# Three-way attention: the scores of the unit two ahead are multiplied between a unit's two turnings, no longer in front of the first

## The chip, the cores and the metric

The kernel runs on one core of a Trainium2 chip. The metric is the device time of one execution in microseconds (us); the median of three executions of the kernel before is 3567.4 us (3563.12 to 3571.15). The core has five engines that run side by side, each strictly in its own program order: TensorE (PE, matmuls), VectorE (DVE), ScalarE (ACT), GpSimd (POOL) and SyncE (SP, which issues the loads). They wait for each other by semaphores.

## The reference, cut to what matters

Two blocks of two layers each run on 512 tokens of width 1024. The change lies in both layers of the second block, in the attention with three branches (compressed keys, selected blocks, window). For each of 8 heads:

```
s_c = q . kc * scale + bias     p_c = masked_softmax(s_c)   o_c = p_c . vc      (31 compressed keys)
s_s = q . ks * scale + bias     p_s = masked_softmax(s_s)   o_s = p_s . vs      (selected blocks)
s_w = q . kw * scale + bias     p_w = masked_softmax(s_w)   o_w = p_w . vw      (window)
o   = g0 * o_c + g1 * o_s + g2 * o_w
```

With 512 tokens there are 8 blocks of 64 and 16 may be selected, so every causal block is selected. All is causal: a block of 128 queries number i reads (i + 1) * 128 keys. The result is multiplied by `w_out`, added to the input and normalised.

## The kernel before, in words

**Units.** The attention stage (`pe_nsa`, `dve_nsa`, `act_nsa`) goes over 16 units u = 4 * hp + i: hp is one of 4 pairs of heads (one head of each of two key groups g), i one of 4 blocks of 128 queries. The number of keys, and with it nearly every duration, grows with i.

**What one unit costs each engine, and the names used below.**

- Scores (PE, `scores(u)`, L1970): six products, in the order compressed 0, selected 1, compressed 1, selected 0, window 1, window 0. They fill banks 0 to 4 of PSUM. Each waits until the same bank's scores of the unit before have been read.
- Reads (DVE, L2176): six passes that add the bias, keep the least value and bring the scores to SBUF. The first one needs the first two products.
- Exponentials (ACT, L2218): six, each after its read.
- Norms (DVE, `post(u)`, L2130 to L2143): a reciprocal, two small products, and four scalings, selected first, window after. They need all six exponentials. In the DVE's program the norms of unit u stand behind the reads of unit u + 1.
- First turning (PE, `turn(u, SLC)`, L1980): 2 * (i + 1) transposes of the selected probabilities into banks 5 and 6. The one of group 0 needs the norm of group 0.
- Second turning (PE, `turn(u, WIN)`, L1980): the same for the window, into the same two banks.
- Copy back (ACT, `back(u)`, L2202): each turned group is copied from its bank to SBUF. A turning waits for the copy back of the turning before it in the same bank, so each turning waits for ScalarE unless something stands between. In the ACT's program the copies back of unit u stand behind the exponentials of unit u + 1.

**What else lies in the stage.** Once in four units, in front of the first turning of i = 3, PE turns the compressed probabilities (`turn_cmp`, L1987), and the DVE copies them (`back_cmp`, L2150) ahead of its reads two units later. Behind the first turning of units 4, 8 and 12, and at the end, PE multiplies a head pair's probabilities by the values (`pv`, L1999 and L2008; 64 products and 8 pairs of short ones); ACT and DVE then take the sum (L2208, L2154). Between the two turnings of units 0, 2, 6, 7, 10, 11, 14 and 15 stands an early part of the output projection (`pe_early2`, L281 to L283, twelve products), which the DVE takes from bank 7 (L2064) behind its reads of the unit two later and in front of its norms, with one to three more passes behind the norms. At u = 4, 9 and 13 ACT makes the high part of a weight slot (L319), and POOL then subtracts to get the low part (L329).

**What sets the order.** All queues are written out by hand; no scheduler moves anything. Ahead of the loop of PE stand scores(0), scores(1) and three quarters of the first early part. The products of the output projection (`pe_out2`) follow the last `pv` at once.

Of the kernel before, what the change touches and what calls it, by code (L numbers as in the profile page):

```python
# [73 lines left out]
def build(nc, t):  # L74
    ctx = ExitStack()
    with ctx:
# [1711 lines left out]
        def pe_hgrn_last(eng):  # L1788
            eng.wait_ge(hsq, HG)
            eng.wait_ge(st_ready, 12)  # L1790
            eng.wait_ge(hrs, 2 * HG - 3)
            eng.matmul(bank[7][:, :], onesD, sq[:, (HG - 1) % 2, :], start=True, stop=True).then_inc(hsum, 1)
# [140 lines left out]
        CMP, SLC, WIN = range(3)  # L1933
# [5 lines left out]
        def cw(i):  # L1939
            return 8 * i + 7  # L1940
# [6 lines left out]
        def score_bank(w, g, m):  # L1947
            if w == CMP:
                return bank[4][:, 64 * g:64 * g + m]
            return bank[2 * (w - 1) + g][:, 0:m]  # L1950

        def pe_nsa(eng):
            eng.wait_ge(tp_free, 13)
            eng.wait_ge(dec_exp, 2 * HU)
            eng.wait_ge(a_mask, A_MASKS * HU)
            eng.wait_ge(hout, HG - 1)

            def scores(u):
                hp, i = divmod(u, NT)
                n = (i + 1) * P  # L1960
                if i == 0:
                    eng.wait_ge(tp_free, 13 + hp)
                for o, (w, g) in enumerate(MADE):
                    lo = g * DH
                    keys = (kcmp[lo:lo + DH, 0:cw(i)], projT[lo:lo + DH, KSL, 0:n], projT[lo:lo + DH, KWI, 0:n])[w]
                    if u:
                        eng.wait_ge(p_max, 6 * (u - 1) + FREED[o])
                    if w == CMP and g == 1:
                        eng.wait_ge(s_ready, 6 * u + 1)
                    eng.matmul(score_bank(w, g, cw(i) if w == CMP else n), projT[lo:lo + DH, NQ + hp, i * P:(i + 1) * P],  # L1970
                               keys, start=True, stop=True).then_inc(s_ready, 1)

            def turn(u, w):
                i = u % NT
                for g in range(2):
                    eng.wait_ge(p_norm, 4 * u + 2 * (w - 1) + g + 1)
                    if u or w == WIN:
                        eng.wait_ge(p_back, 4 * u + 2 * (w - 2) + g + 1)
                    for j in range(i + 1):
                        mm = eng.transpose(bank[5 + g][:, j * P:(j + 1) * P], pslot[u % 3][:, w - 1, g, j * P:(j + 1) * P],  # L1980
                                           ident)
                    mm.then_inc(p_turn, 1)

            def turn_cmp(hp):
                eng.wait_ge(c_norm, 4 * hp + 4)
                for m in range(2):
                    mm = eng.transpose(bank[4][:, (2 + m) * P:(3 + m) * P], pslot_c[:, hp % 2, m, :], ident)  # L1987
                mm.then_inc(c_turn, 1)

            def pv(hp):  # L1990
                eng.wait_ge(p_back, 16 * (hp + 1))
                eng.wait_ge(c_back, hp + 1)
                eng.wait_ge(early_out, EARLY_BEFORE[hp])
                o = bank[7]
                for w in range(2):
                    for j in range(NT):
                        for g in range(2):
                            lo = g * DH
                            eng.matmul(o[lo:lo + DH, j * P:S], vg[:, j, w * P + lo:w * P + lo + DH],  # L1999
                                       pT[g][:, w, j, j * P:S], start=(w == 0 and j == 0), stop=False,  # L2000
                                       skip_group_check=True)
                for i in (0, 2, 1, 3):
                    if i == 1:
                        mm.then_inc(c_half, 1)
                        eng.wait_ge(c_half, hp + 1)
                    for g in range(2):
                        lo, row = g * DH, 64 * (i % 2) + 32 * g
                        mm = eng.matmul(o[lo:lo + DH, i * P:(i + 1) * P], vcmp[row:row + cw(i), 0:DH],  # L2008
                                        probC[row:row + cw(i), hp % 2, i // 2 * P:(i // 2 + 1) * P], start=False,
                                        stop=(i == NT - 1), skip_group_check=True)  # L2010
                mm.then_inc(o_ready, 1)

            scores(0)
            pe_hgrn_last(eng)
            scores(1)
            pe_early2(eng, 0, (0, 1, 2))
            eng.wait_ge(hout, HG)
            for u in range(NU):
                if u + 2 < NU:
                    scores(u + 2)  # L2020
                if u % NT == NT - 1:
                    turn_cmp(u // NT)
                turn(u, SLC)
                if u and u % NT == 0:
                    pv(u // NT - 1)
                if u == 0:
                    pe_early2(eng, 0, (3,))
                if u == 1:
                    eng.wait_ge(early_out, 1)
                    eng.matmul(bank[7][:, :], onesD, early2(0), start=True, stop=True).then_inc(mean_out, 1)  # L2030
                if u in EARLY2_AT:
                    pe_early2(eng, EARLY2_AT.index(u) + 1)
                turn(u, WIN)
            pv(NSA // 2 - 1)
# [8 lines left out]
        def early2(m):  # L2043

            return early[:, m, :] if m < 4 else early_more[:, m - 4, :]

        def pe_early2(eng, m, qs=None):

            if m == 1:
                eng.wait_ge(mean_kept, 1)  # L2050
            elif m:
                eng.wait_ge(early_out, m)
            elif qs[0] == 0:
                eng.wait_ge(hrs, 2 * HG - 1)
            for k, hp in enumerate(range(3)):
                if m == 1 + sum(u < 4 * (hp + 1) for u in EARLY2_AT):
                    eng.wait_ge(o_taken, hp + 1)
            pe_tile(eng, bank[7][:, :], n_out2, A2, m, A2_MADE, [guH[:, HQ + h, :] for h in range(HG)],
                    [guH[:, HGT + h, :] for h in range(HG)], qs)
# [334 lines left out]
        for layer in range(DEPTH):  # L2394
            with nc.Block() as block:
# [28 lines left out]
                @block.tensor  # L2424
                def _(pe):
                    pe_turn(pe, 2)
                    pe_proj_N(pe, n_in2 + 3, (1, 3, 4, 5))
                    pe_compress(pe)
                    pe_turn(pe, 3)
                    pe_compress_out(pe)  # L2430
                    for j in range(4, T2_EARLY - 1):
                        pe_turn(pe, j)
                    pe.wait_ge(vp_free, 4)
                    pe_hgrn_turn(pe)
                    pe_turn(pe, T2_EARLY - 1)
                    pe_hgrn_suffix(pe)
                    pe.wait_ge(k_back, HG)
                    pe_proj_N(pe, n_in2 + 12, HV_BANKS)
                    pe.wait_ge(tp_free, T2_EARLY)
                    pe.wait_ge(suf_exp, 3)  # L2440
                    pe_proj_N(pe, n_vg, VG_BANKS, VG, VG_ROWS, taken=(0, 0, 5, 6),
                              between={0: lambda eng: pe_decays(eng, 0), 1: lambda eng: pe_decays(eng, 1)})
                    pe_hgrn(pe)
                    pe_nsa(pe)
                    pe_out2(pe)
                    pe_layer_norm(pe, 0)
                    pe_ffn(pe, 0, n_ffn2, 8, ln_free(1), norm=1)
                    pe_layer_norm(pe, 1)
                    pair_of(pe, n_next2, 16)
# [289 lines left out]
```

## Time and profile before

| | us |
|---|---|
| median of three executions | 3567.4 |
| the profiled execution's own time | 3564.28 |
| its span in the trace | 3562.5 |
| PE busy in the span | 3421.0 (96%) |
| the attention stage in the first layer of the second block | 119.0, from 2290.5 to 2409.5 |
| the same in the second layer | 119.7, from 3018.7 to 3138.4 |
| PE busy in these two | 104.56 and 105.78 |

A row of the timeline gives the start, the duration of the merged instructions, engine, line, operation and how many; in brackets stands how long the engine was idle before it and what it waited for. A row of the stretches gives the length, busy time and count of each engine in the order PE, weight loads, DVE, ACT, POOL, then the granted TensorE clock as a share of full, the DMA share and GB/s. PE is the engine with the most work in the whole kernel and in the stage; the stage is about 3.3% of the span in each of the two layers.

### The profile page before, as it was taken

To read this page: it belongs to the slowest core of one execution; us is meant where nothing else is said; L and a number is where in the kernel's file an instruction comes from. 1 tells how busy PE (TensorE), PEld (TensorE's weight loads), DVE (VectorE), ACT (ScalarE), POOL (GpSimd) and SP (SyncE) were. 2 spreads that over 40 slices of the span, in tenths; PEclk is the share of its full clock that TensorE was granted. 3 is DMA by queue.
4 is the path that set the end of the run, shared out by engine and by line. 5 is a ranking of instruction groups with operands and counts; after the bars stand their busy time and mean duration, and the time that the engine had idled before them with its cause. 6 is when DMAs were issued, how large, how long until landed. Compare 5 with 4: busy or idle time off the path is not lost. (4 is left out here: it accounts for less than half of the span.)

```text
span 3562.5 us, 47692 instructions
## 1 busy us (share of the span) xinstructions
PE 3421.0 (96%) x17380; PEld 2700.5 (76%) x17380; DVE 1617.5 (45%) x2782; ACT 1270.3 (36%) x2154; POOL 1379.8 (39%) x599
## 2 busy tenths in 40 slices
PE   8999999899999999999999999989999999899998
PEld 6888766688878887766788877757888787568886
DVE  4442345644335432363644155774331458743312
ACT  3222345522232222265322244463222344642223
POOL 3444322244434444222344433304444443034444
PEclk9999999999999999999999999999999999999999
DMA  5333321223323233211223332202323322022332
GB/s 176 97 95 97 116 61 41 65 95 94 99 82 96 95 96 122 83 54 40 79 94 99 97 124 73 67 19 74 98 94 98 122 82 75 13 63 97 96 98 96
DMA packets 86341, 308.18 MB, mean 87 GB/s; under 512 B 11157, under 2 KB 11669, under 8 KB 84798
## 3 DMA queue, kind: packets, MB, share of 16 engines
q1 hardware_dynamic: 86206, 306.37, 27.2%
q8 instruction: 87, 1.43, 0.2%
q14 instruction: 48, 0.39, 0.0%
HBM read 301.59 MB, written 4.74 MB: 86 GB/s over the span
## 5 line engine op out<-in xcount | busy, mean ns | idle before, releaser
L329 POOL TENSOR_TENSOR wL<-ring,wH 128x1024 fp32r<-128x1024 f32 (+1 forms) x519 | 1270.1, 2447 | 2120.3 <-ACT wH L319 2023.6
L281 PE MATMUL bank<-hH,wH 128*128 128x512 f32 x2448 | 965.7, 394 | 11.0 <-DVE yT L758 4.8
L283 PE MATMUL bank<-hH,wL 128*128 128x512 f32 x2448 | 954.3, 390 | 0.0
L282 PE MATMUL bank<-hL,wH 128*128 128x512 f32 x2448 | 953.8, 390 | 0.0
L319 ACT ACTIVATE wH<-ring 128x1024 fp32r<-128x1024 f32 (+1 forms) x525 | 551.2, 1050 | 1122.4 <-PE bank L283 939.5
L281 PEld LDWEIGHTS bank<-hH,wH 128*128 128x128 f32 x2448 | 460.3, 188 | 115.6 <-issue 6.3
L283 PEld LDWEIGHTS bank<-hH,wL 128*128 128x128 f32 x2448 | 460.0, 188 | 96.6
L282 PEld LDWEIGHTS bank<-hL,wH 128*128 128x128 f32 x2448 | 460.5, 188 | 94.6 <-issue 1.4
L281 PE MATMUL bank<-guH,wH 128*128 128x512 f32 x1248 | 492.7, 395 | 2.3 <-ACT early L1154 1.4
L283 PE MATMUL bank<-guH,wL 128*128 128x512 f32 x1248 | 487.4, 391 | 0.0
L282 PE MATMUL bank<-guL,wH 128*128 128x512 f32 x1056 | 410.8, 389 | 0.0
L281 PEld LDWEIGHTS bank<-guH,wH 128*128 128x128 f32 x1248 | 235.6, 189 | 56.8 <-issue 3.2
L283 PEld LDWEIGHTS bank<-guH,wL 128*128 128x128 f32 x1248 | 235.2, 188 | 49.5
L647 DVE TENSOR_TENSOR gfull<-bank,work 128x512 f32<-128x512 f32 x88 | 60.8, 691 | 379.9 <-PE bank L283 379.9
L282 PEld LDWEIGHTS bank<-guL,wH 128*128 128x128 f32 x1056 | 198.2, 188 | 41.8 <-issue 1.0
L654 DVE CAST guH<-gfull 128x512 f32 x132 | 213.1, 1614 | 19.6 <-DVE gfull L652 4.1
L358 DVE TENSOR_TENSOR acc<-acc,work 128x512 f32<-128x512 f32 x36 | 74.8, 2079 | 287.9 <-ACT work L541 287.9
L568 ACT ACTIVATE work<-work 128x512 f32<-128x512 f32 x88 | 55.6, 632 | 416.6 <-DVE work L644 416.6
L656 DVE TENSOR_TENSOR guL<-gfull,guH 128x512 f32 x132 | 182.7, 1384 | 16.2
L652 DVE TENSOR_TENSOR gfull<-work,bank 128x512 f32<-128x512 f32 x44 | 30.3, 688 | 301.4 <-PE bank L283 285.0
L744 PE MATMUL bank<-wH,hH 128*128 128x512 f32 (+1 forms) x320 | 119.9, 375 | 2.4 <-DVE yT L758 2.0
L746 PE MATMUL bank<-wH,hL 128*128 128x512 f32 (+1 forms) x320 | 118.3, 370 | 0.0
(290 smaller groups left out, 3879.2 us busy)
## 6 DMA issues: line engine op xcount, KB each, us to landing
ring<-in_w SPq DMA_DIRECT2D x376, 512.0 KB, 3.6
ring<-in_down SPq DMA_DIRECT2D x96, 448.0 KB, 3.3
ring<-in_down SPq DMA_DIRECT2D x48, 512.0 KB, 3.6
ring<-in_next SPq DMA_DIRECT2D x16, 512.0 KB, 3.6
mix<-in_table SPq DMA_DIRECT2D x2, 2560.0 KB
mix<-spread SPq DMA_DIRECT2D x4, 768.0 KB, 6.3
mix<-row SPq DMA_DIRECT2D x1, 2560.0 KB
spread<-mix SPq DMA_DIRECT2D x1, 2560.0 KB, 7.6
```

The source lines that it names most:

```text
L281: eng.matmul(out, a, hi, start=first, stop=False)
L282: eng.matmul(out, a, lo, start=False, stop=False)
L283: return eng.matmul(out, b, hi, start=False, stop=last)
L319: eng.activation(parts_of(n, per)[0][:, 0:width], ring[:, n % NSLOT, 0:width], ACT.Copy).then_inc(w_hi, 1)
L329: eng.tensor_tensor(l[:, 0:width], ring[:, n % NSLOT, 0:width], h[:, 0:width], ALU.subtract).then_inc(w_lo, 1)
L358: eng.tensor_tensor(acc, acc, sq[:, m % 2, :], ALU.add).then_inc(sq_used, 1)
L568: eng.activation(tmp[:, k, :], src, ACT.Silu).then_inc(silu_ready, 1)
L647: eng.tensor_tensor(full, up, rs, ALU.mult).then_inc(gsteps, 1)
L654: eng.tensor_copy(at_h, full).then_inc(gsteps, 1)
L656: eng.tensor_tensor(at_l, full, at_h, ALU.subtract).then_inc(g_free, 1)
L744: eng.matmul(out, x, a, start=(kc == 0), stop=False)
L746: mm = eng.matmul(out, y, a, start=False, stop=(kc == KD - 1))
```

## The change

Only PE's program differs. In the loop over the units the first turning moves from behind `scores(u + 2)` and `turn_cmp` to the head of the iteration. Nothing is added or left out, no buffer and no wait of any instruction changes, and no other engine's program changes.

```diff
             pe_early2(eng, 0, (0, 1, 2))
             eng.wait_ge(hout, HG)
             for u in range(NU):
+                turn(u, SLC)
                 if u + 2 < NU:
                     scores(u + 2)
                 if u % NT == NT - 1:
                     turn_cmp(u // NT)
-                turn(u, SLC)
                 if u and u % NT == 0:
                     pv(u // NT - 1)
                 if u == 0:
```

On PE, in units 1 and 2, the second turning of unit 1 used to be followed by scores(4) (128 wide) and then by the first turning of unit 2 (three transposes for each group).

```order
 L2030 MATMUL bank7<-early_62,mats_58 128x512
 L1980 MATMUL bank5<-mats_58,mix_73 128x128 x2
 L1980 MATMUL bank6<-mats_58,mix_73 128x128 x2
+L1980 MATMUL bank5<-mats_58,mix_73 128x128 x3
+L1980 MATMUL bank6<-mats_58,mix_73 128x128 x3
 L1970 MATMUL bank4<-mix_73 128x7
 L1970 MATMUL bank1<-mix_73 128x128
```

Now the two turnings, which share banks 5 and 6, follow each other, and the scores come behind them.

On PE, at unit 4, scores(6) (384 wide) used to stand in front of the first turning of unit 4 (one transpose for each group), and the first products with the values (L1999) behind it.

```order
 L1980 MATMUL bank5<-mats_58,mix_73 128x128 x4
 L1980 MATMUL bank6<-mats_58,mix_73 128x128 x4
-L1980 MATMUL bank5<-mats_58,mix_73 128x128 x4
-L1980 MATMUL bank6<-mats_58,mix_73 128x128 x4
+L1980 MATMUL bank5<-mats_58,mix_73 128x128
+L1980 MATMUL bank6<-mats_58,mix_73 128x128
 L1970 MATMUL bank4<-mix_73 128x23
 L1970 MATMUL bank1<-mix_73 128x384
```

Of the two turnings of unit 3 that stood side by side one has gone ahead of scores(5), and the first turning of unit 4 now stands in front of scores(6).

## Rows read from the trace of the kernel before

**Rows 1.** The stretches: both stages, then unit 5 to the early part in each layer, then units 6 to 7.
```profile
2290.50:2409.50 119.00, 104.56 (x653) 67.26 (x652) 80.09 (x335) 75.98 (x268) 15.75 (x10) 0.96 0.12 41
3018.70:3138.40 119.70, 105.78 (x654) 68.94 (x652) 79.31 (x335) 75.72 (x268) 15.66 (x10) 0.94 0.12 41
2332.67:2340.55 7.88, 7.59 (x40) 4.41 (x41) 6.25 (x31) 6.17 (x26) 0.00 (x0) 0.78 0.00 1
3062.30:3068.92 6.62, 5.92 (x40) 3.77 (x41) 5.40 (x27) 5.99 (x26) 0.00 (x0) 1.00 0.01 4
3068.92:3075.19 6.27, 6.27 (x44) 4.97 (x42) 3.75 (x15) 5.75 (x23) 0.00 (x0) 1.00 0.00 1
```

**Rows 2.** The waits of 2290 to 2410 (total us, times, longest), those of PE.
```profile
PE bank L1980 <- ACT mix L2202: 6.7, 8, 1.6
PE bank L1970 <- DVE mix L2176: 3.9, 3, 1.9
PE bank L1980 <- DVE mix L2143: 2.0, 2, 1.7
```

**Rows 3.** Timeline of PE, first layer, units 1 to 5.
```profile
2305.40 2.56 PE L1970 MATMUL bank<-mix 64*128 64x31 f32 x12 [1.25 <-DVE mix L2176]
2307.88 0.66 PE L1980 MATMUL bank<-mats,mix 128*128 128x128 f32 x4
2308.38 1.02 PE L2030 MATMUL bank<-early,mats 128*128 128x512 f32 x2
2310.45 0.69 PE L1980 MATMUL bank<-mats,mix 128*128 128x128 f32 x4 [1.05 <-ACT mix L2202]
...
2325.42 0.53 PE L1980 MATMUL bank<-mats,mix 128*128 128x128 f32 x2 [1.73 <-DVE mix L2143]
2325.88 0.64 PE L1999 MATMUL bank<-mix 128*64 128x512 f32 x1
...
2332.67 0.47 PE L1980 MATMUL bank<-mats,mix 128*128 128x128 f32 x2 [0.96 <-ACT mix L2202]
```

**Rows 4.** Timeline of DVE, first layer: norms 1, early part, norms 3, norms 4.
```profile
2306.69 0.18 DVE L2130 RECIPROCAL mix<-mix 128x6 f32<-128x6 f32 x1
...
2307.22 1.14 DVE L2143 TENSOR_SCALAR mix<-mix 128x256 f32<-128x256 f32 x4
...
2315.90 0.69 DVE L2064 SCALAR_TENSOR_TENSOR early<-xT,bank 128x512 f32<-128x512 f32 x1 [1.98 <-PE bank L283]
...
2317.07 1.67 DVE L2143 TENSOR_SCALAR mix<-mix 128x512 f32<-128x512 f32 x4
...
2320.59 0.42 DVE L2150 COPY mix<-bank 128x256 f32<-128x256 f32 x1
...
2322.70 2.26 DVE L2132 TENSOR_TENSOR mix<-mix 128x6 f32<-128x6 f32 x1
```

**Rows 5.** Timeline of POOL, same stretch: the low part of a weight slot.
```profile
2322.59 2.35 POOL L329 TENSOR_TENSOR wL<-ring,wH 128x1024 fp32r<-128x1024 f32 x1 [21.84 <-ACT wH L319]
```

**Rows 6.** Timeline of PE, second layer, units 4 to 8.
```profile
3062.71 2.54 PE L1970 MATMUL bank<-mix 64*128 64x31 f32 x12
...
3066.49 0.69 PE L1980 MATMUL bank<-mats,mix 128*128 128x128 f32 x4 [0.65 <-ACT mix L2202]
3067.11 1.25 PE L1970 MATMUL bank<-mix 64*128 64x7 f32 x12
...
3081.03 0.44 PE L1980 MATMUL bank<-mats,mix 128*128 128x128 f32 x2
```

**Rows 7.** Timeline of DVE, second layer: first read of unit 7, an early part.
```profile
3063.87 0.69 DVE L2176 CUSTOM_DVE_ANT_0 mix<-bank,mix 128x512 f32<-128x512 f32 x1 [1.16 <-PE bank L1970]
...
3071.97 0.69 DVE L2064 SCALAR_TENSOR_TENSOR early<-xT,bank 128x512 f32<-128x512 f32 x1 [2.45 <-PE bank L283]
```

**Rows 8.** Timeline of ACT, first layer, units 12 and 13.
```profile
2387.57 1.05 ACT L319 ACTIVATE wH<-ring 128x1024 fp32r<-128x1024 f32 x1
...
2392.46 0.39 ACT L2202 ACTIVATE mix<-bank 128x256 f32<-128x256 f32 x1 [0.32 <-PE bank L1980]
```

## The prediction, made before the changed kernel had run

> **What bounds the kernel now.** I read the stretches first. Each attention stage takes 119.0 and 119.7 us, of which PE is busy 104.56 and 105.78, the DVE 80.09 and ACT 75.98 [rows 1]; PE has the most work and about 14 us of idle time. The list of waits says what ends PE's idle time in one stage: 6.7 us in front of turnings for ScalarE's copy back, 3.9 us in front of scores for the DVE's reads, 2.0 us in front of turnings for the norms [rows 2]. So PE is never far from waiting for the other two, and what matters is how work stands between a wait and its releaser. Outside the two stages nothing changes.
>
> The loop that counts: the scores of u + 2 need the reads of u + 1; the norms of u stand behind the reads of u + 1 on the DVE; the first turning of u needs the norms of u; the copy back sits between any two turnings. Before, scores(u + 2) ran while the DVE made the norms of u. Their time (1.25 us for i = 0 and 2.54 for i = 3 [rows 6], of which the last 0.07 overlaps with the next product: 1.2 and 2.5, and by their width 1.6 and 2.0 for i = 1 and 2) covered the norms' 0.9 us to the first scaling's end. Behind the change this cover is gone: PE stands before the norms, and then the DVE stands before the scores.
>
> **The change part by part.** It adds and removes no instruction, so only waits count. I go through one stage in order, with t = when a step starts now against before.
>
> A turn's duration on PE is about 0.2, 0.5, 0.63, 0.79 us (four transposes: 2307.88 to 2308.38 [rows 3]). From the reciprocal to the end of the first scaling is 0.53 + 1.14/4 = 0.82 us for i = 1 (2306.69 and 2307.22), and from the DVE's taking of an early part to the first scaling behind it 2317.07 + 1.67/4 − 2315.90 = 1.59 us for i = 3 [rows 4]. From scores' start to an idle DVE's first read is 1.16 us for i = 3 (3062.71 to 3063.87) [rows 6, 7]; by their width I estimate 0.95, 0.8 and 0.6 us for i = 2, 1, 0.
>
> Unit 0: the first turning waits for nothing new (the early part in front of it covers the norms). 0.
>
> Unit 1: before, PE began scores(3) at 2305.40 [rows 3]. Now it must wait for the norms of 1, whose first scaling ends at 2306.69 + 0.82 = 2307.5 [rows 4]. First turning 2307.6 to 2308.1, scores(3) to 2310.6 instead of 2307.9, the mean's product to 2311.6, ScalarE's guess and copy back, and the second turning at 2312.5 instead of 2310.45: +2.05. The 1.05 us wait that this turning had stays, since the mean's product stands between [rows 3].
>
> Unit 2: its first turning now follows the second one of unit 1 in the same banks; copy back takes 0.39 us plus 0.32 us around it [rows 8], so it starts about 0.85 us after the other began, 2313.35. Scores(4) and the early part follow; its twelve products end 3.05 us after they began (3071.97 − 3068.92 [rows 1, 7]): 2313.35 + 0.63 + 1.2 + 3.05 = 2318.2 instead of 2315.90 [rows 4]. +2.3.
>
> Unit 3: norms 3 stand behind the early part on the DVE: first scaling done at 2318.2 + 1.59 = 2319.8. PE has long finished the second turning of 2 and idles 1.2 us. Before, scores(5) stood here. Then 0.79 + 1.6 + 0.3 (compressed turn): the second turning starts at 2322.5, +2.7. The copy of the compressed turn on the DVE is just in time.
>
> Unit 4: norms 4 were already late: L2132, a product of six columns, took 2.26 us beside POOL's 2.35 us [rows 4, 5], and PE stood 1.73 us [rows 3] after scores(6). POOL's step moves by the 2.7 us of the second turning of 3 and the DVE's reads of 5 by 2.35 us (copy of the compressed turn at 2322.9 instead of 2320.59 [rows 4]), so they still meet, and the first scaling ends about 2327.9, not 2325.3. PE idles from 2323.3 to 2328.0, and only then come the first turning and scores(6), which used to fill the gap. The products with the values start at 2330.4 instead of 2325.88 [rows 3]: **+4.5 us**. Here rows 5 bear on a rule of the Trainium skill, SBUF — State Buffer, section "SBUF: two separate sides": the port pair that VectorE and GpSimd share is an exclusive lock, and the one that starts first keeps it for its whole instruction. By it the small product could slip in front of POOL, since it now has 0.3 us more room. Then the scalings behind it would meet POOL instead, and the sum stays, or all four slip through too, and the sum is 2.2 us a stage less.
>
> Unit 5, counted from the second turning of 4 (zero): copy back 0.7, first turning 0.7 to 1.2, scores(7) 1.2 to 3.7, reads of 7 from 2.36 to 5.06 (four passes of 0.69 less 0.08 overlap each and the two short ones, 2.7 us, by rows 7), norms 6 first scaling 0.53 + 0.35 later (0.35 between 1.14/4 and 1.67/4 [rows 4]), first turning of 6 at 6.0, scores(8) to 7.85, where the early part begins. Before it began at 3068.92 − 3062.30 = 6.62 [rows 1]. **+1.2.** The second turning of 5 sat 0.65 us behind ScalarE [rows 6] and still does; it is not on this chain.
>
> Units 6 and 7, from the start of the early part: its end 3.05, norms 7 first scaling 1.59 behind it at 4.64, first turning 4.7 to 5.5, scores(9) 7.1, compressed turn 7.35. Before 6.27 [rows 1]. **+1.1.**
>
> Unit 8, from the same zero: reads of 9 end 9.5 (behind the compressed copy at 7.5), early part ends 10.4, norms 8 at 11.8, first turning 11.85, scores(10), values at 14.1. Before: 12.6 (3081.03, the first turning [rows 6], and 0.46 to the values as in rows 3, less 3068.92). +1.6 of which 1.1 are told. **+0.5.**
>
> Unit 9: like 5, but ScalarE has 1.05 us of weight work there [rows 8], which held the second turning at 5.3 before as well, so the early part began at 7.8; now at 7.96 by the same chain, at 9.2 if the clock is low while scores(11) runs, as it was before in both layers. I take **+0.8**. Units 10, 11: **+1.1**, unit 12: **+0.5**. Units 13 to 15: no scores are left in 14 and 15, and ScalarE holds the turnings there: 0 to 0.8, taken **0.3**.
>
> Sum of one stage: 4.5 + 1.2 + 1.1 + 0.5 + 0.8 + 1.1 + 0.5 + 0.3 = 10.0 us, in two layers 20.0. Nothing behind the stage hides it: the output projection follows at once on PE.
>
> The clock: the same unit 5 took 7.88 us at a granted clock of 0.78 and 6.62 at 1.00 [rows 1], so a stretch at the lower level (1.2 instead of 2.4 GHz) costs 1.3 us. Two such stretches lie in each stage behind its start. PE's idle time nearly doubles and comes in pieces of 3.4 us (unit 1) and 4.7 us (unit 4), so I add one such stretch per stage: 2.6 us. Bounds: none (0), or three per stage (7.8), which slow the chain where it now runs through the scores. The Trainium skill, TensorE: Matmul & The Clock Gate, section "What's actually happening", says that the throttled state is the default and activity releases it; by that the longer waits are the dangerous ones, which speaks against this change beyond its waits.
>
> Total +22.6 us. Against the profiled execution's 3564.3 us that is 3586.9; it was 3.1 us below the median, so against the median 3590.0.
>
> **The rivals.** (a) Faster: the scores stand between the two turnings and cover the copy back. The eight waits for it make 6.7 us, three of about 0.96 behind the values' products (one in rows 3) remain; 3.8 us a stage, 7.6 in all, 3560. It decides if the norms come in time and the pair second turning, next first turning does not wait instead. Against it: that pair uses the same banks, and the norms cannot come before the reads. (b) No change, 3567: the idle time only moves, since PE had 14 us to give. Against it: in units 6 to 8 PE is busy 6.27 of 6.27 us and the chain there becomes longer than that. (c) Only units 1 to 4 lose, 2 x 4.5 = 9 us, 3576, if the early parts and values cover the rest: the losses of 0.5 to 1.2 us are small sums of estimates. (d) The clock drops in all the new waits: 20 + 2 x 7.8, 3603. It decides if PE's clock is low while scores(3) and scores(6) run.
>
> **How the numbers follow.** Forecast 3590 with 0.67, (a) 0.04, (b) 0.05, (c) 0.12, (d) 0.12. The forecast's own spread: 2.2 us a stage less if norms 4 miss POOL, 0.6 us for unit 9 either way, no clock stretch more (−2.6). That reaches down to about 3580 and up to 3596. For 8 in 10 I go from 3576 (c) to 3602, near (d). About 0.2% (7 us) is what can be told from no change: faster 0.04, same 0.05, slower 0.91.
>
> **What would show it.** Right: each stage is about 130 us long; idle time of PE for L2143 (norms) in front of L1980 rises from 2.0 to over 10 us a stage; the first row L1999 stands about 4.5 us later after the stage's start; the DVE waits for L1970 in most units. The waits of turnings for ScalarE stay within 2 us of 6.7. Wrong: stages under 122 us, or no wait for the norms in units 3 and 8, or waits for ScalarE gone without others in their place.

## The result and the profile after

The changed kernel takes 3606.59 us (median), the one before 3567.93 us over the same stretch of runs: a ratio of 1.0107, interval 1.0090 to 1.0124, or +38.7 us. One of its four executions ran in a slower state (3922.35 us, at a granted clock of 0.84) and is in that median; the other three have a median of 3605.45, +37.5 us. I had forecast +22.6 us, 3590, with a range from 3576 to 3602. The direction held, the size did not: the time lies above the range, near the rival with the lower clock, 3603.

The profiled execution has a span of 3602.9 us against 3562.5, so 40.4 us more. Two stretches hold all of it: the attention stages of the two layers, 138.53 and 140.96 us instead of 119.0 and 119.7 [rows 1]. First the two stages (columns as in rows 1), then the 4 us in which the first layer's scores(7) run.

```profile
2289.17:2427.70 138.53, 112.33 (x653) 72.09 (x652) 80.86 (x335) 75.30 (x268) 15.75 (x10) 0.90 0.11 35
3037.50:3178.46 140.96, 114.64 (x653) 73.14 (x652) 81.14 (x335) 75.34 (x268) 15.68 (x10) 0.89 0.10 35
...
2342.59:2346.60 4.01, 4.00 (x16) 2.58 (x16) 1.17 (x7) 3.55 (x15) 0.00 (x0) 0.57 0.01 2
```

The counts of instructions are those of before, but for one record of PE in the second stage. The granted clock has fallen from 0.96 and 0.94 to 0.90 and 0.89, PE's busy time has risen by 7.8 and 8.9 us for the same work, and its idle time by 11.8 and 12.4 us. The DVE and ACT work as long as before, within 2 us.

Waits of one stage (2290 to 2428; total us, times, longest), which answer to [rows 2], with those of the DVE for scores:

```profile
PE bank L1980 <- DVE mix L2143: 18.5, 13, 3.5
DVE mix L2176 <- PE bank L1970: 15.7, 9, 3.3
...
PE bank L1980 <- ACT mix L2202: 4.0, 7, 1.0
...
PE bank L1970 <- DVE mix L2176: 1.9, 1, 1.9
```

Waits in front of turnings for the norms went from 2.0 to 18.5 us, those for ScalarE's copy back from 6.7 only to 4.0, and those in front of scores from 3.9 to 1.9. The DVE's waits for scores were 4.2 us in the kernel before:

```profile
DVE mix L2176 <- PE bank L1970: 4.2, 5, 1.2
```

PE and the DVE now stand for each other in turn. One of the waits put down to the norms is ScalarE's: the 1.05 us in front of 2314.20 below, when the norms of unit 1 had long been done (they end at 2307.06). The same wait in the second layer is put down to ScalarE:

```profile
3064.60 0.69 PE L1980 MATMUL bank<-mats,mix 128*128 128x128 f32 x4 [1.05 <-ACT mix L2202]
```

So it is rather 17.4 us for the norms and 5.1 for ScalarE.

Timeline of PE, first layer, units 1 to 6, which answers to [rows 3] and [rows 6]:

```profile
2306.33 1.12 PE L1980 MATMUL bank<-mats,mix 128*128 128x128 f32 x4 [3.48 <-DVE mix L2143]
2307.37 4.57 PE L1970 MATMUL bank<-mix 64*128 64x31 f32 x12
2311.87 1.27 PE L2030 MATMUL bank<-early,mats 128*128 128x512 f32 x2
2314.20 0.69 PE L1980 MATMUL bank<-mats,mix 128*128 128x128 f32 x4 [1.05 <-DVE mix L2143]
2315.17 0.85 PE L1980 MATMUL bank<-mats,mix 128*128 128x128 f32 x6 [0.29 <-ACT mix L2202]
...
2321.87 1.09 PE L1980 MATMUL bank<-mats,mix 128*128 128x128 f32 x8 [1.08 <-DVE mix L2143]
...
2327.73 0.33 PE L1980 MATMUL bank<-mats,mix 128*128 128x128 f32 x1 [1.92 <-DVE mix L2143]
2330.02 0.48 PE L1980 MATMUL bank<-mats,mix 128*128 128x128 f32 x1 [1.96 <-DVE mix L2143]
2330.42 3.70 PE L1970 MATMUL bank<-mix 64*128 64x23 f32 x12
2334.05 1.11 PE L1999 MATMUL bank<-mix 128*64 128x512 f32 x1
...
2343.32 3.86 PE L1970 MATMUL bank<-mix 64*128 64x31 f32 x12
2347.11 0.66 PE L1980 MATMUL bank<-mats,mix 128*128 128x128 f32 x4
2349.29 0.88 PE L1980 MATMUL bank<-mats,mix 128*128 128x128 f32 x6 [1.52 <-DVE mix L2143]
```

The reader is to see three things. PE idles 3.48 us for the norms of unit 1, as forecast, and then scores(3) last 4.57 us, which were 2.56 [rows 3]. The same happens at unit 4, where scores(6) last 3.70 us instead of 2.11. And at unit 4 the turning is torn in two: its first transpose starts at 2327.73, its second at 2330.02. The next rows say why. DVE and POOL, same stretch (these answer to [rows 4] and [rows 5]):

```profile
2305.39 0.19 DVE L2130 RECIPROCAL mix<-mix 128x6 f32<-128x6 f32 x1
...
2309.49 0.69 DVE L2176 CUSTOM_DVE_ANT_0 mix<-bank,early 128x512 f32<-128x512 f32 x1 [2.43 <-PE bank L1970]
...
2327.10 0.17 DVE L2132 TENSOR_TENSOR mix<-mix 128x6 f32<-128x6 f32 x1
...
2327.39 2.96 DVE L2143 TENSOR_SCALAR mix<-mix 128x128 f32<-128x128 f32 x4
```

```profile
2327.52 2.36 POOL L329 TENSOR_TENSOR wL<-ring,wH 128x1024 fp32r<-128x1024 f32 x1 [28.09 <-ACT wH L319]
```

The small product now slips in front of POOL (0.17 us, before 2.26), the first scaling too, and the three after it wait for POOL's 2.36 us: four scalings take 2.96 us. This agrees with the exclusive lock on the port pair shared by VectorE and GpSimd that the Trainium skill describes (SBUF — State Buffer, "SBUF: two separate sides"): POOL's instruction ends at 2329.88, and the second transpose starts at 2330.02. The DVE's delay is the same as before, 2.1 us (2.26 − 0.17 and 2.96 − 0.87), only the place differs.

The DVE's first read of unit 3 stands 2.43 us for scores, so the loop is closed: PE waits for norms, then the DVE waits for scores. Two of the signs that I had named for being right came out larger. The stages were to be about 130 us long. The first product with the values (L1999) was to stand about 4.5 us later after the stage's start; it stands 9.5 us later in the first layer (44.88 instead of 35.37 us) and 10.2 in the second.

### The profile page after: what moved, and what is told of

It is laid out like the page before. It is cut to its first block and busy times, and to the rows that moved or that the text cites. A ratio compares the mean times of both kernels' runs of the same rounds, so it can differ in the third digit from the quotient of the medians.

```text
span 3602.9 us, 47692 instructions
## 1 busy us (share of the span) xinstructions
PE 3437.7 (95%) x17380; PEld 2711.8 (75%) x17380; DVE 1619.5 (45%) x2782; ACT 1269.0 (35%) x2154; POOL 1379.1 (38%) x599
## 5 line engine op out<-in xcount | busy, mean ns | idle before, releaser
L281 PE MATMUL bank<-hH,wH 128*128 128x512 f32 x2448 | 965.3, 394 | 11.0 <-DVE yT L758 4.8
L281 PEld LDWEIGHTS bank<-hH,wH 128*128 128x128 f32 x2448 | 460.1, 188 | 115.1 <-issue 6.5
L281 PE MATMUL bank<-guH,wH 128*128 128x512 f32 x1248 | 493.0, 395 | 2.3 <-ACT early L1154 1.4
L281 PEld LDWEIGHTS bank<-guH,wH 128*128 128x128 f32 x1248 | 235.4, 189 | 58.6 <-issue 4.4
```

The lines of the kernel that those rows point to most:

```text
L281: eng.matmul(out, a, hi, start=first, stop=False)
```

## The experiments

All times are medians beside runs of the kernel before on the same chip: 3565.96 us for e1_units0to4, e2_units5on, e3_filled and e4_low_later, 3568.08 for e3b_filled_half, e5_before_low_later, e6_before_filled and e7_split, 3566.08 for e8_filled_low_later to e11_filled_1_and_4. A number with a plus or minus is the difference from that median; for the changed kernel it is +38.7. Two runs are compared by these differences, which are known to within 3 to 6 us each. Fillers are products of two constant matrices, written to a bank that holds nothing at that time, which nobody reads; one takes 0.23 us on PE.

### Which units lose

The first turning goes ahead of the scores in some units only (the diff is against the kernel before):

```diff
+                early_turn = u in (0, 1, 2, 3, 4)
+                if early_turn:
+                    turn(u, SLC)
                 if u + 2 < NU:
                     scores(u + 2)
                 if u % NT == NT - 1:
                     turn_cmp(u // NT)
-                turn(u, SLC)
+                if not early_turn:
+                    turn(u, SLC)
```

> The first turning goes ahead of the scores only in units 0 to 4. The trace of the changed kernel puts +10.5 us per stage before the second turning of unit 4 (9.6 of it before the first product with the values). Theory (long waits at units 1 and 4, with the lower clock and the meeting with POOL behind them): 2 x 10.5 = 21 us over before, 3589. Rival (each of the 14 moved score groups costs the same): 5/14 of 38.7 = 14 us, 3582. My old working (clock and POOL as I had them): 9 us, 3577.

Measured: 3587.44 us, ratio 1.0058 (1.0044 to 1.0071), +21.5. The other half, with units 5 to 15 in that list:

> The first turning goes ahead of the scores only from unit 5 on. If the two parts add up: 38.7 - 21 = 18 us over before, 3586. My old working for these units was 2 x 5.5 = 11 us, 3579. Rival (the late units lose only because the early ones have put the DVE behind): under 5 us, 3572.

Measured: 3585.36 us, ratio 1.0048 (1.0035 to 1.0062), +19.4. The two halves add up to 40.9 against 38.7 for all, so most of the loss is local: each unit pays for its own moved turning. Five units at the head pay as much as the other eleven. It is not all local: in the trace of e1_units0to4 scores(7), (11) and (15), where the order is that of before, take 4.06 to 4.24 us in both layers, in the kernel before only two of the three are slow, and about 2 us of each stage's loss lie there.

### Which part is the clock

```diff
             for u in range(NU):
+                if {1: 28, 3: 4, 4: 30, 6: 8, 10: 8, 14: 8}.get(u, 0):
+                    eng.wait_ge(p_back, 4 * u)
+                    fill(..., 5)
                 turn(u, SLC)
...
+                if {4: 8, 8: 8, 12: 8}.get(u, 0):
+                    eng.wait_ge(p_max, 6 * (u + 2) + 6)
+                    fill(..., 0)
                 turn(u, WIN)
```

> The changed kernel with idle PE filled by products that nobody reads (28 before the first turning of unit 1, 30 before that of unit 4, 4 to 8 before those of 3, 6, 10, 14 and before the second turning behind each product with the values). No wait of the chain goes away. Theory (about 9 us of each stage's loss is the clock's lower level while scores run): scores(3) in 2.5 us instead of 4.6, scores(6) in 2.1 instead of 3.7, total near 3588. Rival (the waits alone cost it, the clock is low where nobody waits): 3606 or more, since fillers only add work.

Measured: 3618.93 us, ratio 1.0149 (1.0135 to 1.0163), +53.0. The forecast of about 3588 missed by my own arithmetic: in fp32 each filler is two passes, 0.23 us, so 28 of them took 6.5 us in a wait of 3.5. Scores(3) ran in 2.54 us nevertheless, as the theory wanted. With fewer (12, 2, 12, 3, 3, 3 and 4, 4, 4):

> As e3_filled, with fewer than half the fillers, since each takes 0.23 us and not the 0.11 I had counted (12 before unit 1's first turning, 12 before unit 4's, 2 or 3 before those of 3, 6, 10, 14, 4 behind each product with the values), so that they fit into the waits. Theory (the clock's lower level costs about 8 us of each stage): scores(3), (6), (7), (11), (15) near 2.5, 2.1, 2.5, 2.5, 2.5 us, total 3591, 15 less than the changed kernel. Rival (a lower clock is cheap, since the scores hide it): 3606.

Measured: 3590.71 us, ratio 1.0061 (1.0048 to 1.0074), +22.6: 16.1 us less than the changed kernel, although PE has 47 fillers more to do in each stage, 10.8 us of work. PE's timeline at units 1 and 4 and then the two stages:

```profile
2306.97 0.70 PE L1980 MATMUL bank<-mats,mix 128*128 128x128 f32 x4
2307.59 2.54 PE L1970 MATMUL bank<-mix 64*128 64x31 f32 x12
...
2328.38 2.11 PE L1970 MATMUL bank<-mix 64*128 64x23 f32 x12
```

```profile
2289.60:2421.00 131.40, 114.21 (x747) 77.41 (x746) 80.28 (x335) 75.35 (x268) 15.79 (x10) 0.99 0.11 37
3030.78:3165.12 134.34, 117.24 (x748) 79.85 (x747) 80.78 (x335) 75.36 (x268) 15.71 (x10) 0.96 0.11 36
```

The scores are back at 2.54 and 2.11 us and the granted clock is 0.99 and 0.96. The turnings start no earlier: that of unit 1 stands 17.4 us after the stage's start, in the changed kernel 17.2. The fillers stand inside the waits. So some 16 us of the changed kernel's time is the lower clock. This is not yet all of it: at the stage's start, where there are no fillers, and from 3114 to 3122 in the second layer the clock is still low (0.53 to 0.62 in the latter). The same treatment of only two places:

> The changed kernel with fillers only before the first turnings of units 1 and 4 (12 each). The traces of the changed kernel and of e3b_filled_half show there 2.0 us for scores(3), 0.7 for the turning and the mean behind, 1.6 for scores(6) and about 1 for the first products with the values. Theory (two thirds of the clock's loss lies in these two places): 2 x 5 = 10 us less than the changed kernel, 3597. Rival (the later scores are slow whatever came before and take as much): 3602 or more.

Measured: 3598.28 us, ratio 1.0088 (1.0074 to 1.0101), +32.2: 6.5 us less than the changed kernel, between the 10 expected and the rival's 4.6 or less; the intervals of the two kernels overlap. In the profiled executions the two stages are 11.1 us shorter together. So the share of units 1 and 4 in the clock's part is not pinned down. The trace shows something that I had not expected. Scores(7) run fast in both layers, with no filler in front of them and the same waits as in the changed kernel:

```profile
2338.61 0.47 PE L1980 MATMUL bank<-mats,mix 128*128 128x128 f32 x2 [0.96 <-ACT mix L2209]
2339.36 0.63 PE L1980 MATMUL bank<-mats,mix 128*128 128x128 f32 x4 [0.29 <-ACT mix L2209]
2339.92 2.54 PE L1970 MATMUL bank<-mix 64*128 64x31 f32 x12
```

Scores(11) stay slow (4.57 and 3.75 us), and scores(15) are slow in the second layer alone. So the waits right in front do not decide alone whether the scores behind the values' products run at the lower clock.

The kernel before has such stretches too, so it was filled in the same way, 8 before scores(1), 7 before the first turning of unit 4, 4 behind each product with the values:

> The kernel before with fillers (8 before scores(1), 7 before the first turning of unit 4, 4 behind each product with the values). Theory (two stretches at the lower clock behind the values cost 1.3 us each where they are not hidden, the one at the stage's start 1 to 2): 2 to 4 us a stage, 3560. Rival (they are hidden or the fillers delay as much): 3566 or more.

Measured: 3562.22 us, ratio 0.9982 (0.9973 to 0.9991), −5.9. Its stages:

```profile
2292.02:2408.23 116.21, 106.14 (x708) 71.63 (x707) 79.25 (x335) 75.38 (x268) 15.78 (x10) 1.00 0.13 42
3019.01:3134.99 115.98, 106.08 (x708) 71.64 (x707) 79.41 (x335) 75.34 (x268) 15.78 (x10) 1.00 0.13 42
```

At a granted clock of 1.00 the order of before needs 116 us a stage. This kernel and e3b_filled_half are the pair by which I compare the two orders below; only this one has fillers at the stage's start.

### Which part is POOL

ScalarE's weight step of unit 4, and with it POOL's, goes one unit later:

```diff
-                if u in (4, 9, 13):
+                if u in (5, 9, 13):
-                    hi(eng, n_out2 + 2 + (4, 9, 13).index(u))
+                    hi(eng, n_out2 + 2 + (5, 9, 13).index(u))
```

> The changed kernel with ScalarE's weight step of unit 4 (and so POOL's) one unit later, behind the products with the values. Theory (POOL keeps the second scaling of unit 4 back by 2 us, and PE stands in the middle of its first turning): 2 x 2.3 = 4.6 us less than the changed kernel, 3602; with PE's wait shorter the clock may keep 1 to 2 us more. Rival (the DVE would not have had the norms earlier, or ScalarE's hour of weight work now holds unit 5): 3606 or more.

Measured: 3599.59 us, ratio 1.0096 (1.0081 to 1.0112), +33.6: 5.1 us less than the changed kernel, which is within the noise of the two; in the profiled executions the two stages are 4.4 us shorter together. The two transposes of unit 4 stand together again and scores(6) last 3.02 instead of 3.70 us, still not 2.1. With the fillers of e3b_filled_half, and 7 instead of 12 at unit 4:

> The changed kernel with fillers (as e3b_filled_half, 7 instead of 12 before unit 4's first turning) and ScalarE's weight step of unit 4 one unit later: the waits of the moved turnings alone, without the lower clock and without POOL. Theory (clock, POOL and waits are separate terms): 3590.7 less 2 x 2.3 = 3586, 18 over before. Rival (POOL's block mattered only through the long idle PE and its clock): 3590.

Measured: 3588.49 us, ratio 1.0065 (1.0051 to 1.0078), +22.4 against +22.6 with POOL's step in its old place, where I expected 4.6 less; the rival holds. The traces hold the reason. In e3b_filled_half the second transpose of unit 4 waited only 0.43 us. With the step moved, the piece to the first products with the values is 1.75 us shorter, and the one behind them, where ScalarE's step now stands, 0.8 longer. The same edit on the kernel before:

> The kernel before with ScalarE's weight step of unit 4, and so POOL's, one unit later. Theory (POOL blocks the DVE's norms of unit 4 for 2.1 us, PE waits 1.73 us for them): 3.4 us less than before, 3563. Rival (scores(6) or ScalarE's exponentials of unit 5 bind next): no change, 3566 to 3567.

Measured: 3566.58 us, ratio 0.9992 (0.9984 to 1.0001), −1.5: no change. And with fillers (8 before scores(1), 4 behind each product with the values):

> The kernel before with fillers (8 before scores(1), 4 behind each product with the values) and the weight step of unit 4 one unit later. Theory (as e6_before_filled, whose 7 fillers in front of unit 4's first turning covered only a wait, less the 1.73 us wait for unit 4's norms): 3562.2 less 2 x 1.7 = 3559. Rival (the step one unit later costs ScalarE as much in unit 5, as e5_before_low_later's unchanged time suggests): 3562 to 3564.

Measured: 3561.68 us, ratio 0.9986 (0.9977 to 0.9995), −4.4, not different from e6_before_filled. Unit 4 does gain (the products with the values start 31.81 us after the stage's start instead of 34.05), and unit 5 gives it back: its second turning now waits for ScalarE, whose weight step stands there.

```profile
2328.95 0.66 PE L1980 MATMUL bank<-mats,mix 128*128 128x128 f32 x4
2331.20 0.68 PE L1980 MATMUL bank<-mats,mix 128*128 128x128 f32 x4 [1.59 <-ACT mix L2211]
```

(Its line numbers are up to 9 higher.) From the values' products to the next early part it takes 14.89 us there, 13.38 in e6_before_filled. Part of this is the clock, which in this trace fell to 0.70 right behind the wait of 1.59 us; the traced execution took 3565.97 us, 4.3 more than the median.

### Scores in two parts

The window's two products between the turnings in units 1, 3, 5, 9 and 13, the first four in front, in the kernel before (scores(u, a, b) makes the products a to b − 1 of the six):

```diff
+                parts = u in (1, 3, 5, 9, 13) and u + 2 < NU
                 if u + 2 < NU:
-                    scores(u + 2)
+                    scores(u + 2, 0, 4 if parts else 6)
                 if u % NT == NT - 1:
                     turn_cmp(u // NT)
                 turn(u, SLC)
+                if parts:
+                    scores(u + 2, 4, 6)
```

> The kernel before with only the last two score products (window) of units 3, 5, 7, 11 and 15 between the two turnings of the unit two earlier; the first four stay in front. Theory (what hurts is that the DVE's first read comes late, not that work stands between the turnings; two products of 0.6 us cover the copy back of 0.3 to 0.6 us): 1 to 2 us a stage less than before, 3563. Rival (any score behind a turning costs): 3570 or more.

Measured: 3577.16 us, ratio 1.0028 (1.0019 to 1.0037), +9.1. My theory fell: even a third of the scores behind the turning costs. In the first layer of its trace the first turning of unit 1 now waits 0.55 us for the norms, the one of unit 6 0.18 us, and stretches at a lower clock lie at units 2 (0.83 and 0.75) and 14 (0.57), where there were none. How the 9 us divide between these I did not settle. The other way round, the first two products in front and four behind, in all units (this diff is against the changed kernel, the list of units is cut):

```diff
+                parts = u in (0, 1, ..., 15) and u + 2 < NU
+                if u + 2 < NU:
+                    scores(u + 2, 0, 2 if parts else 6)
                 turn(u, SLC)
-                if u + 2 < NU:
-                    scores(u + 2)
+                if parts:
+                    scores(u + 2, 2, 6)
                 if u % NT == NT - 1:
                     turn_cmp(u // NT)
```

> The first two of the six score products (compressed 0, selected 1) go back in front of the first turning in all units, the other four stay behind it. Theory (half of the loss is that the DVE's first read waits for the scores, and PE gets 0.5 to 1 us of work into each wait for the norms): about half of the 38.7 us, 3586. Rival (what costs is all that is left behind the turning; the reads of the DVE then stand for the third product as they stood for the first): 3600 or more.

Measured: 3600.96 us, ratio 1.0093 (1.0077 to 1.0108), +34.9, only 3.8 us less than the changed kernel and not told from it by the noise; the rival holds. At unit 1 the DVE's wait for its first read is gone, but it now stands for later products (0.38 and 1.12 us), and the clock is low for longer than in the changed kernel, through units 1 and 2. Four stretches of 4 us:

```profile
2306.00:2310.00 4.00, 3.14 (x12) 1.66 (x12) 3.54 (x19) 2.58 (x12) 0.00 (x0) 0.56 0.02 4
2310.00:2314.00 4.00, 4.00 (x8) 1.17 (x4) 2.43 (x10) 0.00 (x0) 0.00 (x0) 0.50 0.00 0
2314.00:2318.00 4.00, 2.95 (x11) 1.65 (x11) 1.59 (x7) 2.58 (x8) 0.00 (x0) 0.50 0.00 0
2318.00:2322.00 4.00, 4.00 (x18) 3.13 (x17) 1.09 (x12) 3.50 (x13) 0.00 (x0) 0.50 0.01 2
```

## Why the prediction was right in its waits and wrong in its sum

**The loop: right.** That the first turning waits for the norms, the norms for the reads, and the reads then for the scores shows in the waits (18.5 and 15.7 us) and in their places: 3.48 us at unit 1, 1.08 at unit 3, 1.92 and 1.96 at unit 4, 1.52 at unit 6. I had said 3.4 us for unit 1, 1.2 for unit 3 and 4.7 for unit 4, and nothing for unit 6. Waits for ScalarE fell by 1.6 us (6.7 to 5.1), within the 2 that I had allowed, and the waits for norms grew beside them, so rival (a) had nothing to gain; rival (c), only the head loses, is refuted by the units from 5 on, which cost 19.4 us alone.

**The wait terms: 10.0 us a stage forecast, 13.6 measured.** The comparison is the pair of filled kernels, from their traces, in the first layer; a piece begins where the one before it ends; times in us. (Distances are between the first products of the early parts, L281, and of the values, L1999.)

| piece | e6_before_filled | e3b_filled_half | more | forecast |
|---|---|---|---|---|
| second piece of the early part in unit 0 to the first values, units 1 to 4 | 22.94 | 28.12 | 5.2 | 4.5 |
| values to early part, units 4 to 6 | 13.38 | 14.97 | 1.6 | 1.2 |
| early part to early part, unit 7 | 6.26 | 7.60 | 1.3 | 1.1 |
| to the next values, unit 8 | 6.20 | 7.01 | 0.8 | 0.5 |
| values to early part, units 9 to 10 | 14.37 | 15.77 | 1.4 | 0.8 |
| early part to early part, unit 11 | 6.27 | 7.60 | 1.3 | 1.1 |
| to the next values, unit 12 | 6.21 | 7.00 | 0.8 | 0.5 |
| values to the stage's end, units 13 to 15 | 29.47 | 30.63 | 1.2 | 0.3 |
| sum | | | 13.6 | 10.0 |

The first row runs from the second piece of the early part in unit 0 (11.11 and 12.70 us after the start) to the first values (34.05 and 40.82). What lies ahead of it is 1.6 us longer in e3b_filled_half, but at the lower clock, which the changed kernel shares with the kernel before. In the second layer the same pieces are 16.6 us longer; 3.0 of this lies in units 9 to 11, where the clock of e3b_filled_half fell, and 13.6 is left there too. In e8_filled_low_later, whose clock stays at 1.00 behind the start in both layers, the sum is 12.6 and 12.7. Each term came out short, by 0.2 to 0.9 us; in unit 7, for one, the first turning takes 1.03 us to the scores behind it in the changed kernel, where I had 0.79. What made the others short I did not measure. The measured waits also contain what of the fillers does not fit into a wait, so 13.6 is an upper value.

**The failed step: the clock's term.** I wrote "I add one such stretch per stage: 2.6 us", bounded at three. By the medians of the filled kernels the lower clock costs the kernel before 5.9 us in all and the changed one 16.1 us, so the change brings 10 us, uncertain by some 8, and rather more than less, since e3b_filled_half keeps some stretches at the lower clock that e6_before_filled does not have. By the traces it brings what the waits leave, 40.8 − 27.2 = 13.6 us. I had 2.6. In the changed kernel scores(3), (6), (7), (11) and (15) all ran slow in both stages (4.57, 3.70, 3.86, 3.80 and 3.71 us in the first), in the one before two of the five in each. That is three more per stage, my upper bound, and each costs more than the 1.3 us that I had read from unit 5 (2.3, if the 13.6 us are spread over all six). I take it that this is so because the scores are now on the chain: scores(3) alone lost 2.0 us and the turning in front of it 0.5. I had named that mechanism in the bounds, given it 0.12, and taken the price from one pair of stretches of the unchanged kernel. Its total, 3603, came near the measured time in part by luck: the bound of 7.8 us already holds both layers (three times two times 1.3), and rival (d) takes it twice; once, it gives 3595. What speaks for counting it fully was in the trace of the kernel before: I forecast idle pieces of 3.4 and 4.7 us, and there 0.59 and 1.94 us of idle time at the stage's start already have a lower clock (0.83 and 0.74) at and behind them:

```profile
2294.00:2298.00 4.00, 2.68 (x14) 1.79 (x15) 3.69 (x25) 3.51 (x18) 3.86 (x5) 0.83 1.06 406
2298.00:2302.00 4.00, 4.00 (x17) 2.81 (x18) 2.96 (x9) 1.90 (x10) 2.61 (x3) 0.74 0.47 185
```

The rule of the Trainium skill, TensorE: Matmul & The Clock Gate, "What's actually happening" (throttled is the default, activity releases it) pointed there. The traces agree with it: fillers that nobody reads brought the clock to 0.99 and 0.96 and the time down.

**POOL.** "They still meet" was right, at another instruction. The step moved the loss from the front of the norms to between the first and the second scaling, where it splits a turning: the second transpose stands 40.85 us after the stage's start, where I had the whole turning at 37.5. Taken away in the changed kernel it gave 5.1 us (4.4 in the stages of the traces), in the filled one 0.2, in the kernel before 1.5, none of them clear of the noise. If the 5.1 us are real, most of POOL's price in the changed kernel was the longer idle time, after which the clock was low, and not the block itself. This is inferred from the three differences; the runs do not show it directly.

Sum: 27.2 us of waits (forecast 20.0) and 13.6 us of clock (forecast 2.6) make the 40.8 us by which the two stages grew; the clock's part is the remainder, not a measurement of its own. Either miss alone would have left the time inside my range (3597 or 3601). It took both to leave it.

A version that beats both is e6_before_filled or e9_before_both: 0.14 to 0.18% below the kernel before. The first of them keeps the old order and only keeps PE busy in its waits.

## What to carry to other kernels

When a producer's work (here the scores for two units ahead) stands in front of a wait, it hides the wait; put behind it, it makes the other engine wait in its turn. Ask of each moved piece which wait it was covering. When a forecast leaves the matrix engine idle for some microseconds, price what runs behind the wait at half the clock, above all if it is on the chain: scores(3) took 4.57 us behind 3.48 us of idle time, and 2.54 with fillers in it. A wait that can't be removed can be filled with work that nobody reads, if the fillers are shorter than the wait: with 12 in front of unit 1's first turning, and the other places filled as lightly, the changed kernel gained 16.1 us; with 28 there it lost 14.3.

## What I had not expected of the hardware

- New idle time of PE came with more busy time for the same instructions: the two stages have 24.2 us more of the one and 16.6 us more of the other, 40.8 in all.
- Scores behind the products with the values run slow with only 0.95 and 0.29 us of waits there (the clock was 0.57 for the 4 us from 2342.59). With 4 fillers, 0.93 us, in the first of these waits scores(7) took 2.54 us, but so they did in e11_filled_1_and_4, with the same waits, no filler there and fillers at units 1 and 4 alone. What decides it lies further back, and no run shows what it is.
- A 128-column product in fp32 of the filler's kind took 0.23 us in two passes of 0.12, so 28 of them 6.52 us.
